# The recurrence's score-value product half a step later, and the order of two DVE instructions per level

## What the reference computes

```python
def step(state, inp):                      # one chunk, one direction
    b = jnp.cumsum(lfx, axis=2)
    decay = jnp.exp(jnp.where(causal, b[t] - b[s], -jnp.inf))
    scores = jnp.einsum('bhtk,bhsk,bhtsk->bhts', qx, kx, decay)
    o = jnp.einsum('bhts,bhsv->bhtv', scores, vx) + ...   # and the carried state
...
o = o_f + o_b                              # forward and backward in time
o = o * lax.rsqrt(jnp.mean(o * o, axis=-1, keepdims=True) + NORM_EPS)
return o * norm_gain * silu(gate)
```

## Time and profile before

| | before |
|---|---|
| median of 3 executions | 2150.7 us (2150.51 to 2152.18) |
| the profiled execution: its own time | 2152.27 us |
| its span, first to last instruction | 2150.5 us |
| PE busy | 2133.7 us (99%) |
| PEld busy | 1768.1 us (82%) |
| DVE busy | 1557.7 us (72%) |
| POOL busy | 1249.4 us (58%) |
| ACT busy | 1062.7 us (49%) |
| mean granted TensorE clock | 0.998 of full speed |
| read from memory | 397.80 MB |

### The profile page before, as it was taken

The page is one execution under the profiler, slowest core; times in us unless marked ns, Lnnn a source line. Parts: engine busy times, 40 slices in busy tenths (PEclk is TensorE's granted clock), DMA queues, the critical chain, the costliest instruction groups (busy, mean ns, idle before and its releaser), DMA issues.

```text
span 2150.5 us, 28852 instructions
## 1 busy us (share of the span) xinstructions
PE 2133.7 (99%) x11598; PEld 1768.1 (82%) x11598; DVE 1557.7 (72%) x2192; ACT 1062.7 (49%) x1040; POOL 1249.4 (58%) x583
## 2 busy tenths in 40 slices
PE   9999999999999999999999999999999999999998
PEld 7888888888888887888888888888888888878887
DVE  7872789898876786555388737898898767865653
ACT  6444444446566654434454434345566565644442
POOL 4455544336785867666534555443366867666664
PEclk9999999999999999999999999999999999999999
DMA  8555545345455454655565555453554544546554
GB/s 323 194 195 196 176 160 193 140 185 184 176 180 184 167 182 171 255 195 190 185 222 190 192 195 176 159 193 137 193 180 175 179 181 170 187 166 250 191 191 151
DMA packets 59764, 403.86 MB, mean 188 GB/s; under 512 B 6768, under 2 KB 6896, under 8 KB 12272
## 3 DMA queue, kind: packets, MB, share of 16 engines
q1 hardware_dynamic: 59488, 401.49, 52.0%
q10 hardware_dynamic: 144, 0.52, 0.1%
HBM read 397.80 MB, written 4.19 MB: 187 GB/s over the span
## 4 chain that ended last, share of the span: by engine, by line
PE 75%; DVE 13%; POOL 5%; issue 3%; ACT 3%; DMA 1%; DVEq 0%; POOLq 0%; ACTq 0%
PE acc L1282 70%; PE side L1282 4%; DVE w_lo L490 4%; DVE arena L951 2%; POOL w_lo L490 2%; POOL arena L618 1%; ACT w_hi L487 1%; DVE arena L1107 1%; POOL arena L615 1%; DVE wide L951 1%; POOL arena L616 1%; DMA raw<-w_stream 1%; DVE arena L1102 1%; DVE arena L1076 0%; DVE arena L1067 0%
## 5 line engine op out<-in xcount | busy, mean ns | idle before, releaser
L490 POOL TENSOR_TENSOR w_lo<-raw,w_hi 128x768 fp32r<-128x768 f32 x367 | 1019.4, 2778 | 855.4 <-ACT w_hi L487 844.3
L487 ACT ACTIVATE w_hi<-raw 128x2048 fp32r<-128x2048 f32 x366 | 701.0, 1915 | 873.3 <-PE acc L1282 855.0
L490 DVE TENSOR_TENSOR w_lo<-raw,w_hi 128x1280 fp32r<-128x1280 f32 (+1 forms) x371 | 613.7, 1656 | 511.1 <-ACT w_hi L487 508.0
L1282 PE MATMUL acc<-w_hi,xT_hi 128*128 128x512 f32 x2112 | 654.6, 393 | 0.3 <-DVE w_hi L996 0.2
L1282 PE MATMUL acc<-w_hi,xT_lo 128*128 128x512 f32 x2112 | 648.3, 390 | 0.0
L1282 PE MATMUL acc<-w_lo,xT_hi 128*128 128x512 f32 x2112 | 526.3, 391 | 0.0
L1282 PEld LDWEIGHTS acc<-w_hi,xT_lo 128*128 128x128 f32 x2112 | 396.7, 188 | 83.8 <-DVE xT_lo L451 0.2
L1282 PEld LDWEIGHTS acc<-w_lo,xT_hi 128*128 128x128 f32 x2112 | 393.9, 188 | 82.0 <-issue 0.2
L1282 PEld LDWEIGHTS acc<-w_hi,xT_hi 128*128 128x128 f32 x2112 | 393.1, 188 | 79.9 <-DVE w_hi L996 0.4
L951 DVE STREAM_TRANSPOSE arena<-stage 32x256 f32<-32x256 f32 (+1 forms) x480 | 204.8, 427 | 7.0
L1107 DVE TENSOR_TENSOR arena<-arena 128x512 f32<-128x512 f32 x64 | 84.9, 1326 | 30.7 <-ACT arena L855 30.7
(11 more groups left out here) (147 smaller groups left out, 1940.3 us busy)
## 6 DMA issues: line engine op xcount, KB each, us to landing
raw<-w_stream SPq DMA_DIRECT2D x366, 1024.0 KB, 4.8
x_out<-arena SPq DMA_DIRECT2D x16, 256.0 KB, 3.0
arena<-x_turned_in SPq DMA_DIRECT2D x4, 514.0 KB, 7.6
arena<-x_in SPq DMA_DIRECT2D x2, 1024.0 KB, 14.7
arena<-x_in SPq DMA_DIRECT2D x4, 512.0 KB, 6.2
wide<-post_in SPq DMA_DIRECT2D x2, 1024.0 KB, 6.9
arena<-x_out SPq DMA_DIRECT2D x4, 512.0 KB, 5.7
raw<-w_stream SPq DMA_DIRECT2D x3, 512.0 KB, 7.3
```

The costliest lines, as they stand in the source:

```text
L487: return act.activation(w_hi[:, g % ROUNDED, :], raw[:, g % LANDING, :], ACT.Copy)
L490: return eng.tensor_tensor(w_lo[:, g % LANDING, cols], raw[:, g % LANDING, cols], w_hi[:, g % ROUNDED, cols].bitcast(F32), ALU.subtract)
L1282: return pe.matmul(out, a, b, start=start, stop=stop)
```

## The change

PE's 16 matmuls of scores and values move out of the end of step d = 15 into a function `rec_outs`, called between `hi_pass` and `lo_pass` of step d = 16, behind `level_grams`. What follows each of them (ACT's squares, POOL's root, DVE's multiplication by root and gate) moves from d = 16 and 17 to d = 17 and 18, and the last entry of `TURN_C` from 143 to 144, with it the reload of the input by a step. In every level DVE makes q's product ahead of the copy of the level before; before it was the other way round.

```diff
-TURN_C = [Z_A_END + 1, Z_A_END + 3, REC[3] + 5, REC[3] + FIRST_LEVEL + 11]
+TURN_C = [Z_A_END + 1, Z_A_END + 3, REC[3] + 5, REC[3] + FIRST_LEVEL + 12]
...
-                            if s == REC[u] + FIRST_LEVEL + 9:
+                            if s == REC[u] + FIRST_LEVEL + 10:
 
                                 pool.wait_ge(S.rec_squared, u + 1)
...
-                            if d == FIRST_LEVEL + 9:
+                            if d == FIRST_LEVEL + 10:
                                 act.wait_ge(S.rec_out, u + 1)
...
+                                if l < LEVELS:
+
+                                    dve.wait_ge(S.decays, LEVELS * u + l + 1)
+                                    dve.tensor_tensor(decayed_q(l), q, EQ[:, 0], ALU.mult).then_inc(S.mixed, 1)
+                                if l >= 1:
                                     src = side[0][:, (nine + l - 1) % 2 * 512:(nine + l - 1) % 2 * 512 + 512].rearrange(
                                         "p (b t) -> p b t", t=P)
...
-                                if l < LEVELS:
-
-                                    dve.wait_ge(S.decays, LEVELS * u + l + 1)
-                                    dve.tensor_tensor(decayed_q(l), q, EQ[:, 0], ALU.mult).then_inc(S.mixed, 1)
...
-                            if d == FIRST_LEVEL + 10:
+                            if d == FIRST_LEVEL + 11:
                                 dve.wait_ge(S.rec_rstd_ready, u + 1)
...
+                def rec_outs(s):
+
+                    for u in range(4):
+                        _, _, v, _, _, j = rec_views(u)
+                        if s == REC[u] + FIRST_LEVEL + 9:
+                            pe.wait_ge(S.kept, (LEVELS + 1) * (u + 1))
+                            evacuated(pe, S, CHUNKS.index(("c_v", u // 2, KT)))
+                            if u:
+                                pe.wait_ge(S.rec_y, u)
...
+                            ins.then_inc(S.rec_out, 1)
...
                         level_grams(s)
+                        rec_outs(s)
                         lo_pass(s, [0, 1]).then_inc(pe_step, 1)
...
-                            if d == FIRST_LEVEL + 8:
-                                pe.wait_ge(S.kept, nine + LEVELS + 1)
...
-                                ins.then_inc(S.rec_out, 1)
```

More of the change, by code:

```diff
@@ L1407, in level_grams @@
                         ins.then_inc(S.grams, 1)
+                def rec_outs(s):
[6 more added lines that the diff above has]
+                                pe.wait_ge(S.rec_y, u)
+                            for h in range(2):
+                                for tt in range(MT):
+                                    i = h * MT + tt
+                                    o = side[1][:, i * P:(i + 1) * P]
+                                    mm(o, S_diag[:, i], v[:, tt, (j + h) * HD:(j + h + 1) * HD], stop=False)
+                                    ins = mm(o, S_off[:, h * MT + 1 - tt], v[:, 1 - tt, (j + h) * HD:(j + h + 1) * HD],
+                                             start=False)
+                            ins.then_inc(S.rec_out, 1)
                 pe.wait_ge(warm_ready, 1)
```

## The result

The changed kernel is slower. Its median is 2158.19 us (2156.98 to 2158.47, 7 runs), that of the kernel before in the same comparison 2152.18 us (2150.51 to 2152.82, 7 runs). The ratio is 1.0027, 95% interval 1.0018 to 1.0036. 2148.1 was predicted, with a range up to 2151.5. The three runs shown at first had a median of 2150.7, and the four that came to them lie at 2152.06 to 2152.82.

What follows compares the result with a forecast made beforehand. PE, busy 2133.7 of 2150.5 us, was taken to set the end. Median 2150.7 - 6.4 (moved product) + 3.9 (order) + 0 gave 2148.2, the profiled execution 2148.0; both were called 2148.1, range 2143.5 to 2151.5.

Steps and rivals of the forecast that it cites:

- What bounds the kernel: PE sets the end, busy 2133.7 of 2150.5 us; at most 16.8 us of idle time can be won.
- The moved product: Score-value matmuls behind `hi_pass`: the `S_off` wait goes in all eight units, -6.4 us, or -8.2 with the fallen clock.
- What follows the product: Squares, root, multiplications, unit 3's transposes and input reload one step later: priced at 0, between 0 and +1 us.
- The median as an execution without a fallen clock: Kernel before: median 2150.7 us taken as without the clock loss of about 1.8 us, the profiled 2152.27 as with it.
- The order in unit 3: Levels 2 and 4: product still held behind POOL, copy then comes behind it; +0.65 us in all per layer.
- The order in unit 0: 0.15 us lost at level 2, more lateness in later levels; +0.6 us per layer, between 0.15 and 2.
- The order in unit 2: Level 6: product ends behind POOL as before, copy comes after it; +0.7 us per layer.
- Rival C: DVE's lateness piles up, each level from 2 to 7 adding 0.65 us: 2157 us; chance 0.07.
- Rival B: q's product gets ahead of POOL and the copy behind it costs nothing: 2144.3 us, or 2141.9; chance 0.33.

Runs made afterwards that it cites:

- the first experiments: Four kernels: the move alone 2143.62 us; the order alone 2163.56; the changed kernel with unit 2 in old order 2146.92; with transposes six steps later 2166.52.
- level 5 alone: The move in the old order, with q's product ahead of the copy only at unit 2's level 5: 2149.89 us, ten executions 2143.81 to 2153.66.

## Why the prediction was wrong

**What bounds the kernel: right.** PE's busy time is 2133.7 and 2133.8 us, and what separates the kernels is waits of PE in the recurrence and the clock behind them, but for 0.1 us per moved product.

**The moved product: right, a little small.** -6.4 us was predicted and -8.2 with the clock. The move alone measured 2143.62 against 2150.74 us, 7.1 us less. By the traces it is 7.2 us of waits and 1.6 us of clock. What follows the product, priced at 0, cost nothing that shows.

**The median as an execution without a fallen clock: wrong here.** Seven runs have a median of 2152.18, so the forecast of 2148.1 started 1.5 us too low for this comparison. Executions of the kernel before lie mostly near 2150.7 or near 2152.2, and which of the two holds the median changes from set to set: it is 2150.74 in the 15 runs beside the first experiments.

**The order in unit 3: right.** +0.65 us per layer was predicted by way of the product held up behind POOL. Measured +0.57 and +0.73. The profile showed what was named: a product longer by what it was issued earlier (2.25 for 1.70 us), and PE waiting for the masked copy.

**The order in unit 0: right within its bounds.** +0.6 predicted, +0.78 measured in each layer, all at level 2, where 0.15 was expected. The expected 0.15 took the product for a clean 0.68 us. In the changed kernel it meets POOL's line 616 and ends 0.55 us behind it:

```profile
531.86 1.97 POOL L616 TENSOR_TENSOR arena<-arena 128x256 f32<-128x256 f32 x1
...
533.16 1.22 DVE L1099 TENSOR_TENSOR arena<-arena 128x512 f32<-128x512 f32 x1
534.30 0.72 DVE L1107 COPY_PREDICATED arena<-lmasks,side 128x512 f32<-128x512 uint8 x1
```

That the total of the unit came out near the forecast is luck.

**The order in unit 2: the step that failed.** "I take +0.7, as DVE's copy of level 3 may leave it a little late by then." It was 3.7 and 4.0 us of wait and 1.4 and 1.0 us behind it, about 10 us in all where 1.4 stood in the sum. These 8.7 us are most of the 10.1 between forecast and measurement, and they turn a small gain into a loss. The local cost of level 6 was sized well (0.8 with only the even levels turned). What was missed is level 5, where PE waits for nothing. There the copy had cost DVE nothing, as it ran while ACT made the exponential, and the `aT_lo` pair behind the product had just 0.65 us in hand before POOL's line 618. The copy, now behind the product, took exactly that. I had worked through what each product of q stands behind, but not what the other two-input instructions behind it on DVE would meet once they start later. Level 3, which I did name, costs next to nothing by itself (0.17 us of PE per layer).

**Rival C** gave 2157, against 2158.19 measured, with a chance of 0.07. Its direction was right, and that unit 2 pays more than a copy. Its mechanism, 0.65 us added by each level from 2 to 7, was not: most of the lateness comes in one jump, 1.30 us at the pair of level 5 and 1.09 at the `w_lo` behind it. It had 2.9 us for unit 0 and 2.9 for unit 2, where 0.8 and about 5 were measured per layer, so that its 2157 comes so near is luck. The reason given against it, that DVE and POOL would change places and the lateness stop, is what happens in unit 2 at level 3 to 4, and the reverse is what happens at level 5.

**Rival B** (0.33) needed products that get ahead of POOL. They did not shrink where POOL ran (2.25 us for 1.70), and the waits came back.

**Open:** whether the tie at level 5 ever falls the other way in the changed kernel itself. In its trace it falls against DVE in both layers, and its seven runs lie within 1.5 us, while those of level 5 alone spread over nearly 10. Why the two kernels differ in this no run shows.

## What to carry to other kernels

Before two instructions of a queue are turned round, find what each stands still behind: an instruction that costs nothing because it runs while another engine holds up the next one becomes a full charge when it goes second. Then follow the queue on from there, past the last instruction that anyone waits for, and note for each that can be held up how much it has in hand before its rival starts; a slip of the size of that margin costs the rival's whole duration and not its own. When a change has two independent parts, time them apart: here one gained 7 us and the other lost 13.

## What the runs showed of the hardware

DVE instructions with two inputs in SBUF and POOL's on SBUF run one after the other, whole: `aT_lo` pairs of 0.86, 2.07 and 3.37 us, `w_lo` of 1.49, 1.60 and 2.69, q's product of 0.68, 1.70, 2.25, each by where POOL was. Masked copies out of PSUM took 0.71 to 0.75 us in all of these places. The Trainium skill has this as a rule ("SBUF — State Buffer", Who interferes with whom: of two such instructions the one issued first runs whole and the other stands still), and the rows agree but for near ties. The first of the pair in the changed kernel took 1.37 us, against 0.47 with POOL idle, though its record starts 0.01 us ahead of POOL's line 618. So it was in all eight places with a start 0 to 0.03 us ahead: at such a distance the start in the record does not say who goes first.

TensorE's clock fell to the lower level behind a wait of 3.87 us in unit 2, and in one of two waits of 1.88 us in the kernel before; it stayed at 1.00 through all of unit 3 once the longest wait was 1.27 us.
